# Products with no use ahead of the turns of each norm, in a two-block model kernel

## What is computed

```python
# first block, DEPTH 2: each layer is SwiGLU half, mixer, SwiGLU half, each behind an RMS norm
x = x + 0.5 * swiglu(rmsnorm(x, g), w_gate, w_up, w_down)
x = x + mixer(rmsnorm(x, g), ...)          # layer 0: even_mixer, layer 1: odd_mixer
x = x + 0.5 * swiglu(rmsnorm(x, g), ...)
x = rmsnorm(x, final_norm_w)
# second block, DEPTH 2
h = layer_norm(x, ln_in_g, ln_in_b)
for layer in range(2):
    proj = h @ w_in[layer]                 # retention, HGRN2 and windowed attention follow
    h = layer_norm(ALPHA * h + mix, ...)
    ff = swiglu_2(h, ...) if layer == 0 else moe_swiglu(h, ...)
    h = layer_norm(ALPHA * h + ff, ...)

def rmsnorm(x, g):
    y = x * lax.rsqrt(jnp.mean(x * x, axis=-1, keepdims=True) + RMS_EPS)
    return y * g
```

## Time and profile before

| | |
|---|---|
| median of 3 runs | 3223.09 us (3223.01 to 3228.24) |
| profiled execution | 3222.68 us, span of the profile 3220.9 us |
| mean granted TensorE clock | 0.977 |
| TensorE (PE) busy | 3062.6 us, 95% |
| VectorE busy | 2410.0 us, 75% |
| ScalarE busy | 1797.8 us, 56% |

### The profile page before, as it was taken

The page is one execution under the profiler, slowest core; times in us unless marked ns, Lnnn a source line. Parts: engine busy times, 40 slices in busy tenths (PEclk is TensorE's granted clock), DMA queues, the critical chain, the costliest instruction groups (busy, mean ns, idle before and its releaser), DMA issues. The chain is left out here.

```text
span 3220.9 us, 45769 instructions
## 1 busy us (share of the span) xinstructions
PE 3062.6 (95%) x18298; PEld 2680.8 (83%) x18298; DVE 2410.0 (75%) x2718; ACT 1797.8 (56%) x2123; POOL 189.6 (6%) x101
## 2 busy tenths in 40 slices
PE   7998999998999899999998999998999999999997
PEld 6887788876688899899888998997888888888886
DVE  5656666898766666675767567657999999999998
ACT  4445544433244455454444455545877877877876
POOL 0001000002400002110000021100000000000000
PEclk9998999999999999999999999998999999999999
DMA  5552355443155533344554433446999999999995
GB/s 196 184 196 95 118 191 204 171 169 118 66 183 184 199 136 130 134 171 145 183 191 162 144 135 133 168 145 228 368 363 358 363 356 364 361 357 355 365 371 215
DMA packets 97703, 698.64 MB, mean 217 GB/s; under 512 B 10992, under 2 KB 11504, under 8 KB 14064
## 3 DMA queue, kind: packets, MB, share of 16 engines
q1 hardware_dynamic: 97520, 696.11, 58.6%
HBM read 693.97 MB, written 1.05 MB: 216 GB/s over the span
## 5 line engine op out<-in xcount | busy, mean ns | idle before, releaser
L879 PE MATMUL ps<-weight_high,act_parts 128*128 128x512 f32 (+2 forms) x1760 | 463.2, 348 | 10.9 <-DVE act_parts L1913 2.3
L850 PE MATMUL ps<-act_parts,weight_high 128*128 128x512 f32 x1760 | 459.5, 395 | 8.5 <-DVE weight_low L705 8.5
L658 ACT ACTIVATE weight_high<-ring 128x2048 fp32r<-128x2048 f32 x108 | 206.6, 1914 | 310.8 <-PE ps L850 232.3
L850 PEld LDWEIGHTS ps<-act_parts,weight_high 128*128 128x128 f32 x1760 | 319.1, 190 | 69.0 <-DVE weight_low L705 11.2
L879 PE MATMUL ps<-act_parts,weight_low 128*128 128x256 f32 x1312 | 372.8, 284 | 0.0
L879 PEld LDWEIGHTS ps<-weight_high,act_parts 128*128 128x128 f32 x1760 | 310.3, 192 | 55.1 <-issue 9.2
L705 DVE TENSOR_TENSOR weight_low<-ring,weight_high 128x2048 fp32r<-128x2048 f32 x108 | 247.3, 2290 | 126.9 <-ACT weight_high L658 126.9
L879 PE MATMUL ps<-weight_low,act_parts 128*128 128x256 f32 (+2 forms) x1008 | 339.5, 337 | 0.0
L879 PE MATMUL ps<-act_parts,weight_high 128*128 128x256 f32 x1792 | 331.7, 287 | 3.0 <-DVE weight_low L2555 2.9
L2555 DVE TENSOR_TENSOR weight_low<-ring,weight_high 128x2048 fp32r<-128x2048 f32 x82 | 196.1, 2396 | 157.8 <-PE ps L879 142.9
L879 PEld LDWEIGHTS ps<-act_parts,weight_high 128*128 128x128 f32 x1792 | 281.9, 193 | 7.1 <-DVE weight_low L2555 4.3
(11 more groups left out here) (453 smaller groups left out, 6457.5 us busy)
## 6 DMA issues: line engine op xcount, KB each, us to landing
ring<-in_l_moe_up SPq DMA_DIRECT2D x110, 1024.0 KB, 5.4
ring_more<-in_l_moe_down SPq DMA_DIRECT2D x110, 1024.0 KB, 5.3
ring<-in_l_w_in SPq DMA_DIRECT2D x92, 1024.0 KB, 4.8
vtm<-in_l_moe_gate SPq DMA_DIRECT2D x55, 1024.0 KB, 5.8
merged<-in_l_moe_gate SPq DMA_DIRECT2D x55, 1024.0 KB, 5.7
ring<-in_l_ffn_down SPq DMA_DIRECT2D x52, 1024.0 KB, 4.8
ring<-in_l_ffn_up SPq DMA_DIRECT2D x35, 1024.0 KB, 4.8
ring_more<-in_l_ffn_gate SPq DMA_DIRECT2D x32, 1024.0 KB, 4.8
```

The costliest lines, as they stand in the source:

```text
L658: nc.scalar.activation(highs[slot], raws[raw], ACT.Copy).then_inc(high.sem, 1)
L850: return c.nc.tensor.matmul(c.ps[:, bank, :], still, c.act[:, k, :, :].rearrange("p s t -> p (s t)"), start=k == 0, stop=k == KD - 1, skip ...
L879: ins = nc.tensor.matmul(out, still[a], moving[b], start=first and n == 0, stop=last and n == 2, skip_group_check=True)
```

## The change

Ahead of the turns, TensorE runs a number of products of 128 stationary columns by 512 moving columns. Both operands are the rounded part of the next unit, as it lies in `weight_high`, and the result goes to PSUM bank 3. Nothing reads it. The number is 15 for every RMS norm, 38 for the joined final norm, 32 for the layer norm ahead of the second mixer of the second block, 23 for the one ahead of its dense SwiGLU. The first norm of the program has no unit split ahead (`rounded` is None), and gets none.

```diff
@@ Rms.__init__
         self.c, self.gain = c, gain
+        self.products, self.rounded = 15, rounded_ahead(c)
@@ LayerNorm
-    def __init__(self, c, rows, columns):
+    def __init__(self, c, rows, columns, products):
         self.c, self.rows = c, rows
+        self.products, self.rounded = products, rounded_ahead(c)
@@ FinalLayerNorm
-        super().__init__(c, rows, columns)
+        super().__init__(c, rows, columns, 38)
@@
+def keep_running(c, norm):
+    for _ in range(norm.products if norm.rounded is not None else 0):
+        c.nc.tensor.matmul(c.ps[:, 3, :], norm.rounded[:, 0:P], norm.rounded[:, 0:512], start=True, stop=True)
+
+def rounded_ahead(c):
+    return c.weight_high[:, c.high_order[0], :] if c.split_ahead else None
+
 def norm_turns(c, norm, pe, rows):
+    keep_running(c, norm)
     for h in range(2):
         for t in range(TT):
             pe.wait_ge(norm.normed.sem, norm.normed.base + 2 * h + t + 1)
@@ second_layer
-        norm = LayerNorm(c, (d["ln_ffn_g"][0], d["ln_ffn_b"][0]), columns(2))
+        norm = LayerNorm(c, (d["ln_ffn_g"][0], d["ln_ffn_b"][0]), columns(2), 32)
@@
-        norm = LayerNorm(c, (d["ln_mix_g"][0], d["ln_mix_b"][0]), columns(1))
+        norm = LayerNorm(c, (d["ln_mix_g"][0], d["ln_mix_b"][0]), columns(1), 23)
```

## The result

| | before | changed |
|---|---|---|
| median | 3223.14 us (6 runs, 3223.00 to 3228.24) | 3236.05 us (6 runs, 3234.56 to 3237.33) |
| ratio | | 1.0034, 95% interval 1.0024 to 1.0044 |
| profiled execution, span | 3220.9 us | 3232.8 us |
| mean granted clock | 0.977 | 0.983 |

The change makes the kernel slower by 0.24 to 0.44%; the medians are 12.9 us apart, the spans of the two profiled executions 11.9. I had forecast 3226.0, with 3217 to 3233, so the measured time lies outside, and 72% stood on "no change". Yet the page shows what the change wanted: the clock is up.

The account below looks back on a forecast made before the run. The prediction took TensorE, busy 95% of the span, as the bound. Overruns less clock gains at eight first units summed to +3.1 us, which with the profiled 3222.68 and 0.4 to the median gave 3226 us, range 3222 to 3230 (8 in 10: 3217 to 3233).

Parts of the forecast that it names:

- the pace of a product: Added products ahead of the norms' turns: each takes 0.2267 us, so 15 take 3.40 us and 32 take 7.25.
- the full clock at seven norms: At seven of eight touched norms, products, turns and first unit run at full clock, as pauses of about 1.71 us hold it.
- the turns: TensorE's turns of the norm's rows, behind the products: sixteen in about 1.9 us, against 3.40 us at half clock.
- the chain that paces the SwiGLU units: In three touched SwiGLU stages ScalarE and VectorE pace the first unit's first half, so the clock costs it almost nothing.
- the ends of eight first units: Change in when the first unit behind each touched norm ends, from -1.3 us (even) to +2.65 (second mixer); together +3.1 us.
- the overrun: Products past the room between stage begin and first turn delay the turns: 0.46 to 2.50 us per norm.
- the second mixer's norm: Layer norm with 32 products: overrun 2.50 us, clock falls in half of executions (+0.8 us on the mean), +2.65 us in all.
- Nothing is issued on other engines, no DMA, no semaphore: The products add work to TensorE alone; no cost was counted elsewhere.
- All other work of each stage follows its first unit: Stages stand one behind the other, so the first units' +3.1 us is carried whole to the kernel's end.
- The first: Rival: products fit into the room ahead of the turns, so the clock comes free; 6.4 us gained, 3216.7 us; chance 0.07.
- The second: Rival: clock falls in the pause before the products, which run at half clock; up to +12 us, 3238 us; chance 0.14.
- The third: Rival: clock still falls at the turns or they don't speed up; 5.2 us more, 3231 us; chance 0.05.

Follow-up runs that it names:

- rms20: Changed kernel with 20 products instead of 15 ahead of each RMS norm, the others as they were; 3235.43 us in one execution.
- before_again: The kernel before, unchanged, profiled a second time; 3228.84 us in one execution.
- pad_start: Kernel before plus 40 tiny products of zeros (80 instructions) in the first stage; 3228.88 us, 1.0012 of the kernel before.
- after_aligned: Changed kernel plus 88 tiny products of zeros in the first stage, making 512 instructions more than the kernel before; 3233.61 us, 1.0026 of the kernel before.
- fit_mixer13: Changed kernel with 10 products per RMS norm, 32 for the joined final norm, 13 for the second mixer's, 20 for the dense SwiGLU's; 3219.97 us, 0.9983 of the kernel before.

## Why the prediction was wrong

**Right:** the pace of a product (0.228 us on the mean against 0.2267; 0.235 in a row of 15, whose first ones are slower), their start with the stage (0.05 us behind SyncE's first DMA), the full clock at seven norms, the turns (0.11 us apart; sixteen in 1.9 us), the chain that paces the SwiGLU units, and so the ends of eight first units: +4.2 against +3.1. That last agreement is partly luck, since the prediction had one execution of the kernel before, and against the other it is +1.7: the turns of two norms, which the prediction took as quick, were so because the clock happened to fall late (in the third SwiGLU stage only the first few; the sixteen took 3.00 us). That the overrun is passed on whole within the SwiGLU stages also held; rms20 doubles it and finds it in each.

**Mis-sized:** the second mixer's norm. I gave its fall of the clock half a chance, +0.8; it came in every profile with that pause, and the whole norm costs 3.5 us instead of 2.65. Against before_again it costs 2.7, for there the clock of the kernel before fell 0.2 us ahead of this stage and not 0.8 behind its begin.

**The steps that failed:** First, "Nothing is issued on other engines, no DMA, no semaphore", and no more was asked of the instructions: the sum had no term for TensorE's code. 336 more instructions made a branch wait for a fetch, 2.8 us. pad_start and after_aligned show it by itself. Second, "All other work of each stage follows its first unit ... so I carry it whole to the end". The SwiGLU stages did carry it; the mixers, whose clock falls later on for reasons of their own, did not always. In the mixer of layer 0 it is +2.7 us on top of +0.5. In three of three profiles with the 38 and 15 it is there, and in the one with six products less it is gone. My account, that a shift of 1 us moves the stage's pauses against the stretches at half clock, fits these profiles but isn't shown by itself: rms20 has the same 38 and 459.8 us, and the kernel before has the 462 in one profile of two without any product.

That makes 4.2 + 2.8 + 2.7 = 9.7 of the profile's 11.9 us, or 6.6 of the 8.8 us by which it lies above the forecast's 3.1. The rest is +0.7 in the first stage, which has no products, and +1.7 in the even mixer behind its first unit, less some. These stages last 199.3 to 200.6 and 146.5 to 151.1 us in twelve profiles, with no order by kernel that I could see, so I take them for the scatter of one execution. That isn't shown. The split holds for this pair of profiles alone. In the second pair, 3236.74 against 3228.84 us, the mixer of layer 0 adds nothing, the first units add 1.7, the branch 2.8, and the odd mixer 2.4 (135.6 against 133.2 us), none of it in its first unit. What both pairs share is the branch, and that mixers last longer or shorter than their first units say. Why the changed kernel comes into the mixer of layer 0 in the same way each time stays open, and so does how much of the 12.9 us between the medians is chance in these places.

**The rivals:** The first (products fit, all gain, 6.4 us) named the mechanism of the good version. Its first units gain 2.2, 0.85, 0.1, 1.4, 0.1, 0.65, 0.65 and 0.6 us in fit_mixer13, together 6.5, about as computed (6.4); of these 4 to 5 come out at the end. The second (clock at half in every pause) didn't come; one norm of eight. The third fell: in the changed kernel every turn behind the products stands 0.11 us from the next, against 0.21 at half clock. The clock also rose in the kernel before while nothing but turns was running: at 1088.70 the last two of sixteen stand 0.11 us apart, after 9.3 us of pause and 3 us of turns. So the measurement differs from what the Trainium skill says in "TensorE: Matmul & The Clock Gate", Part 4 on the PE-mode transpose, that the full clock does not engage for transposes.

## What to carry to other kernels

Work that only keeps the clock up must end before what it waits beside is ready: here each product past that made the first unit end later by its full time, while the clock gives back no more than half of the time that dependent matmuls run at the low level. Count it from the barrier and not from the last product, and where a pause is too long to be bridged, expect the first products at half pace. Adding instructions ahead of a jump over unused code can cost microseconds by their number alone; try the same kernel with the code shifted before the time is put down to what the instructions do. And profile the kernel before more than once: one execution's falls of the clock decide what each stage seems to gain or lose.

## What the runs showed of the hardware

- TensorE's jump over a long unused body takes 0.36 to 0.47 us (with 0, 230, 244, 268 or 512 instructions more ahead of it) or 2.96 to 3.98 us (with 80, 324, 336 or 386 more). In the longer ones a 16 KB instruction packet runs during the jump, and the whole core waits.
- In every profile of a kernel with the products, the clock held through pauses of 1.0 to 1.8 us that were followed by them; in each that kept the pause of 3.2 us it fell 0.3 to 1.5 us behind the stage's begin, for 3.4 us. There 512 columns take 0.43 us.
- With one code a stage takes 458.8 or 462.1 us, with 17.1 or 23.9 us of it at half clock; another takes 131.5 or 135.6, with 6.8 or 17.1.
- Turns by TensorE stand 0.11 us apart at full clock and 0.21 at half, and the clock rose while nothing but turns ran.
